# Moving the sample's early gate products in a two-layer diffusion backbone on one NeuronCore

## What is computed

```
proj = h @ w_in
attn = attention(...)                        # 8 heads
z    = short_conv(hy_in, width 3)            # 1536 channels: v, x1, x2 (512 each)
y    = v
for o in (0, 1):
    y = z[o + 1] * long_conv(y, filter[o])   # bidirectional, by a Fourier transform
g_a, g_b = split(sigmoid(gates))             # gates: 2 x 1024 columns of proj
merged = g_a * (attn @ w_oa) + g_b * (y @ w_ob)
x = x + gate1 * (merged @ w_out)
x = x + gate2 * peer(norm(x))                # 128 experts per token, fetched by index
```

## Time and profile before

| | us |
|---|---|
| median of three runs | 4868.67 |
| span of the profiled execution, first to last instruction | 4858.6 |
| median less span, what lies around it | 10.1 |
| TensorE busy | 3814.1 |
| VectorE busy | 3260.8 |
| layer 0, short convolutions begin to last gate product | 728.9 to 1106.3 |
| layer 1, the same | 2997.8 to 3360.0 |

### The profile page before, as it was taken

How to read it: one execution, slowest core, us unless ns; L and a number is a source line. 1 busy time by engine, 2 the same in 40 slices (tenths; PEclk the granted TensorE clock), 3 DMA queues, 4 the chain that set the end, 5 groups by cost and what they waited for, 6 DMA issues and landing times.

```text
span 4858.6 us, 42229 instructions
## 1 busy us (share of the span) xinstructions
PE 3814.1 (79%) x12642; PEld 2042.6 (42%) x12642; DVE 3260.8 (67%) x7651; ACT 1557.8 (32%) x4562; POOL 1793.3 (37%) x1515
## 2 busy tenths in 40 slices
PE   7987788797798766767877679799699777777776
PEld 4546464445454223323543346445555332322222
DVE  2323788858867986666567778876877876755555
ACT  2321241101234344434333323110233444444444
POOL 2330132333234434455344323224233444444443
PEclk8889889898899889898989889899799999999999
DMA  7565376766799989999999767766689999999998
GB/s 269 203 225 202 136 272 256 272 242 260 314 372 384 391 332 422 398 411 385 395 416 421 295 231 267 289 230 272 248 352 359 412 405 415 418 414 421 421 421 347
DMA packets 231264, 1602.62 MB, mean 330 GB/s; under 512 B 27558, under 2 KB 29906, under 8 KB 42876
## 3 DMA queue, kind: packets, MB, share of 16 engines
q0 software_dynamic: 198016, 1395.87, 72.4%
q1 hardware_dynamic: 33020, 204.06, 10.8%
HBM read 1588.52 MB, written 11.30 MB: 329 GB/s over the span
## 4 chain that ended last, share of the span: by engine, by line
PE 38%; DMA 28%; DVE 21%; issue 5%; ACT 5%; POOL 2%; SPq 0%; ACTq 0%; DVEq 0%; POOLq 0%
DMA sb_arena<-in_peer_uv,sb_idx 15%; PE ps L1133 14%; DMA sb_gbufs<-in_peer_uv,sb_idx 10%; PE ps L1029 7%; DVE sb_gbufs L1929 4%; PE ps L1070 4%; DVE sb_arena L1929 3%; DVE sb_eacc L1952 2%; PE ps L717 2%; PE ps L744 2%; PE ps L887 1%; DMA sb_ring<-in_w_oab 1%; DVE sb_arena L1915 1%; ACT sb_small L1393 1%; POOL sb_gbufs L2172 1%
## 5 line engine op out<-in xcount | busy, mean ns | idle before, releaser
L2172 POOL DMA_INDIRECT sb_gbufs<-in_peer_uv,sb_idx x768 | 981.9, 1279 | 1783.7 <-PE ps L1133 758.4
L1133 PE MATMUL ps<-sb_gbufs,sb_dge 128*128 128x512 f32 x1856 | 912.3, 641 | 281.5 <-ACT sb_dge L1413 274.0
L1133 PE MATMUL ps<-sb_arena,sb_dge 128*128 128x512 f32 x1856 | 902.4, 636 | 267.2 <-ACT sb_dge L1413 267.0
L2172 POOL DMA_INDIRECT sb_arena<-in_peer_uv,sb_idx x512 | 610.3, 1192 | 789.4 <-PE ps L1133 691.7
L1929 DVE CUSTOM_DVE_ANT_0 sb_gbufs<-sb_gbufs,sb_keep 128x1024 f32<-128x1024 f32 x512 | 625.6, 1235 | 355.7 <-DMA sb_gbufs<-in_peer_uv,sb_idx 352.5
L1929 DVE CUSTOM_DVE_ANT_0 sb_arena<-sb_arena,sb_keep 128x1024 f32<-128x1024 f32 x512 | 622.1, 1229 | 327.0 <-DMA sb_arena<-in_peer_uv,sb_idx 325.0
L1133 PEld LDWEIGHTS ps<-sb_gbufs,sb_dge 128*128 128x128 f32 x1856 | 363.1, 204 | 793.0 <-issue 392.3
L1133 PEld LDWEIGHTS ps<-sb_arena,sb_dge 128*128 128x128 f32 x1856 | 360.8, 202 | 777.2 <-issue 390.5
L1390 ACT ACTIVATE sb_small<-sb_small 128x2 f32<-128x2 f32 x512 | 104.1, 203 | 1516.3 <-DVE sb_small L1929 1491.1
L1952 DVE SCALAR_TENSOR_TENSOR sb_eacc<-sb_gbufs,sb_small,sb_eacc 128x1024 f32<-128x1024 f32 x299 | 387.3, 1295 | 7.8 <-DVE sb_small L1962 0.3
L1397 ACT ACTIVATE sb_small<-sb_small 128x1 f32<-128x1 f32 x1024 | 340.6, 379 | 49.6 <-ACT sb_small L1393 2.2
(11 more groups left out here) (272 smaller groups left out, 4276.7 us busy)
## 6 DMA issues: line engine op xcount, KB each, us to landing
sb_ring<-in_w_wq SPq DMA_DIRECT2D x48, 1024.0 KB
sb_keep<-in_w_ada POOLq DMA_DIRECT2D x52, 512.0 KB, 6.1
sb_ring<-in_w_hy SPq DMA_DIRECT2D x24, 1024.0 KB
sb_ring<-in_w_ga SPq DMA_DIRECT2D x16, 1024.0 KB
sb_ring<-in_w_gb SPq DMA_DIRECT2D x16, 1024.0 KB
sb_ring<-in_w_oab SPq DMA_DIRECT2D x16, 1024.0 KB
sb_ring<-in_w_out SPq DMA_DIRECT2D x14, 1024.0 KB
sb_gbufs<-in_peer_uv,sb_idx POOLq DMA_INDIRECT x768
```

Source lines behind the costliest of these rows:

```text
L1133: q = pe.matmul(ps[:, c, :], dge[:, b, :], gbuf[b][:, D + c * 512:D + c * 512 + 512], start=(h == 0 and i == 0), stop=(h == HALVES - 1 and ...
L2172: nc.gpsimd.indirect_dma_start(out=gbuf[b], out_offset=None, in_=I["peer_uv"], in_offset=bass.IndirectOffsetOnAxis(ap=idx[:, col:col + 1], ...
```

## The change

It changes the sample's dense steps alone.

- The first turning waits for four slices, not for eight, and comes after blocks 0 to 2 of the short convolution. Block 3 follows the first turning.
- The early gates (g_a and attn @ w_oa for c = 0, 1) come after the first inverse transform, before the second turning. Their tanh waits for the four results of the first order.
- Beside the second spectrum stand the products for g_b of c = 0 and 1 instead (new `early_second_gates`, banks 4 and 6), with their tanh.
- The gate step c = 0 then has the products of column 2 for g_a and g_b and (0, 3); step 1 has (1, 3) alone; step 2 has (2, 2) and (2, 3). The banks of the gate steps are shifted by four.
- Spectra 0 and 2 go to the arena too, and the load order is new. `w_oab` of columns 0 and 1 is loaded twice, the second time as `ob`: one more load of 1 MB for each layer.
- `pace` has new numbers; their sum falls from 933.8 to 899.8 us.

```diff
+def products_at(g, c):
+    if not g.latent or c > EARLY:
+        return [(c, q) for q in range(4)]
+    ahead = [(EARLY, 0), (EARLY, 1)]
+    return (ahead if c == 0 else []) + ([(c, 3)] if c < EARLY else [(c, 2), (c, 3)])
...
     def merge_bank(self, c, v):
-        return (4 * c + v) % 8 if self.latent else 2 + (4 * c + v) % 6
+        return (4 * c + 4 + v) % 8 if self.latent else 2 + (4 * c + v) % 6
...
-        at = [20 * k] + ... + [4.5] * (NH * nt) + [10] + [8 * k + 2] * (8 if self.latent else 12)
-        for o in (0, 1):
-            if self.latent:
-                at += [10] + [3.6] * 4 + ([10.5] * EARLY if o else [8] * 4) + [6] * 4
...
+        at = [20 * k] + ... + [4.5] * (NH * nt) + [10] + [8 * k + 2] * (6 if self.latent else 12)
+        if self.latent:
+            at += [4] + [8] * 2 + [3.6] * 4 + [8] * 4 + [3.5] * 4 + [10.5] * EARLY + [4] + [3.6] * 4 + [7.5] * EARLY + [3.5] * 4
...
-        return at + ([12] * EARLY + [21 * k + 2] * (8 - EARLY) if self.latent else ...
+        return at + ([20, 6, 8] + [21 * k + 2] * 5 if self.latent else ...
...
-            out += hy[0:4] + conv("MF", 0, "U_ps", 2) + conv("K", 0, "Ym", 1) + hy[4:5] + conv("K", 1, "Ym", 2, half) + hy[5:6]
-            out += conv("MI", 0, "y_ps", 4) + conv("MF", 1, "U_ps", 4) + conv("K", 2, "Ym", 3) + conv("K", 3, "Ym", 4, half)
-            out += [gates[0][0], gates[0][2]] + conv("MI", 1, "y_ps", 8) + [gates[0][1]]
+            out += hy[0:4] + conv("MF", 0, "U_ps", 2) + conv("K", 0, "Ym", 1, first) + conv("K", 1, "Ym", 2, half) + hy[4:6]
+            out += conv("MI", 0, "y_ps", 4) + [gates[0][0], gates[0][2]]
+            out += conv("MF", 1, "U_ps", 4) + conv("K", 2, "Ym", 3, first) + conv("K", 3, "Ym", 4, half)
+            out += [gates[0][1]] + conv("MI", 1, "y_ps", 8) + [((d, "ob", 0), 2048, None, free("mg_ps", gates_at(g, 1, 3)))]
...
-                yield from short_convolution(range(4 if g.latent else 6))
+                yield from short_convolution(range(3 if g.latent else 6))
...
-                    if g.latent:
-                        pe.wait_ge(*at("hyc", 12 if o else 8))
-                    else:
-                        pe.wait_ge(*at("hyc", 12))
+                    pe.wait_ge(*at("hyc", 4 if g.latent else 12))
...
+                def early_second_gates():
+                    pe.wait_ge(*loaded((d, "gb", 0)))
+                    w = weights((d, "gb", 0), 256)
+                    for c in range(EARLY):
+                        claim(4 + 2 * c, *at("eb_th", c + 1))
+                        for k in range(KD):
+                            m = pe.matmul(ps[:, 4 + 2 * c, :], w[:, k, c * 128:c * 128 + 128], v.hT[:, k, :], start=(k == 0), stop=(k == 7))
+                        m.then_inc(s["eb_ps"], 1)
+                        yield
...
                     turn_u(o)
                     yield
+                    if o == 0:
+                        yield from short_convolution((3,))
...
-                    if o:
-                        yield from early_gates()
-                    else:
-                        yield from short_convolution((4, 5))
+                    yield from early_second_gates() if o else short_convolution((4, 5))
...
+                    if o == 0:
+                        yield from early_gates()
...
+                    if g.latent and o == 0:
+                        act.wait_ge(*at("y", 4))
+                        for c in range(EARLY):
+                            act.wait_ge(*at("ea_ps", 2 * c + 1))
+                            act.activation(v.early[:, c, :], ps[:, 4 + 2 * c, :], ACT.Tanh, scale=0.5).then_inc(s["ea_th"], 1)
+                            yield
...
-                        if c >= 2:
-                            act.wait_ge(*at("mm", c - 1))
+                        if g.latent and cp < EARLY + 2:
+                            act.wait_ge(*at("y", 5 + 2 * (cp % 2) + q))
+                        elif cp >= 2:
+                            act.wait_ge(*at("mm", cp - 1))
```

More of the change, by code:

```diff
@@ L43 @@
 EARLY = 2
+def products_at(g, c):
[3 more added lines that the diff above has]
+    return (ahead if c == 0 else []) + ([(c, 3)] if c < EARLY else [(c, 2), (c, 3)])
 def gate_products(g):
-    return [(c, q) for c in range(KD) for q in range(4) if not (g.latent and c < EARLY and q % 2 == 0)]
+    return [p for c in range(KD) for p in products_at(g, c)]
 def gates_at(g, c, q):
@@ L169, in weight_loads @@
         hy = [((d, "hy", i), 2048, None, free("hyc_ps", 2 * i + 2)) for i in range(6)]
-        gates = [[((d, "ga", i), 2048, None, free("ea_ps", 3) if g.latent and 2 * i < EARLY else free("mg_ps", gates_at(g, 2 * i + 1, 0))),
-                  ((d, "gb", i), 2048, None, free("mg_ps", gates_at(g, 2 * i + 1, 1))),
-                  ((d, "oab", i), 2048, None, free("mg_ps", gates_at(g, 2 * i + 1, 3)))] for i in range(4)]
+        gates = [[((d, "ga", i), 2048, None, free("ea_ps", 3) if g.latent and i == 0 else free("mg_ps", gates_at(g, 2 * i + 1, 0))),
+                  ((d, "gb", i), 2048, None, free("eb_ps", 2) if g.latent and i == 0 else free("mg_ps", gates_at(g, 2 * i + 1, 1))),
+                  ((d, "oab", i), 2048, None, free("ea_ps", 4) if g.latent and i == 0 else free("mg_ps", gates_at(g, 2 * i + 1, 3)))] for i in range(4)]
         if g.latent:
@@ L1270, in short_convolution @@
                         yield
-                yield from short_convolution(range(8 if g.latent else 12))
+                yield from short_convolution(range(6 if g.latent else 12))
                 for o in (0, 1):
@@ L1715, in spectrum_s, with early_gates @@
                         yield from short_convolution(range(8, 12))
+                def early_gates():
+                    for c in range(EARLY):
+                        dve.wait_ge(*at("ea_th", c + 1))
+                        dve.wait_ge(*at("ea_ps", 2 * c + 2))
+                        dve.scalar_tensor_tensor(out=v.early[:, c, :], in0=v.early[:, c, :], scalar=1.0, in1=ps[:, 5 + 2 * c, :],
+                                                 op0=ALU.add, op1=ALU.mult).then_inc(s["ea"], 1)
+                        yield
                 for o in (0, 1):
@@ L1751, in dense @@
                 for c in range(KD):
-                    for q in (0, 1):
-                        if (c, q) not in gate_products(g):
-                            continue
-                        dve.wait_ge(*at("th", tanhs_at(g, c, q)))
+                    early = g.latent and c < EARLY
+                    for q in ((1,) if early else (0, 1)):
+                        dve.wait_ge(*(at("eb_th", c + 1) if early else at("th", tanhs_at(g, c, q))))
                         dve.wait_ge(*at("mg_ps", gates_at(g, c, 2 + q)))
@@ L2083, in dense @@
                     if g.latent:
-                        for _ in range(5 + (EARLY if o else 4)):
+                        for _ in range(5 + EARLY if o else 1 + 2 + 4 + 4):
                             yield
@@ L2094, in dense @@
                         yield
-                    for _ in range(4):
+                    for _ in range(4 + (EARLY if g.latent and o == 0 else 0)):
                         yield
```

62 lines of the change are left out of this document (31 added, 31 removed).

## The result

The changed kernel takes 4844.35 us (median of four runs, 4840.91 to 4856.21) and the kernel before 4869.34 beside it: the ratio is 0.995, with a 95% interval of 0.9932 to 0.9967. So it is faster, by 25.0 us. Run once more later it had 4850.21 against 4871.03, ratio 0.9954 (0.994 to 0.9967), which is 20.8 us. Both intervals stay clear of 1; between them they allow a gain of 16 to 33 us. The prediction was 4839.0 with a range of 4814 to 4861.

The account below looks back on a forecast made before the run. The stage was taken as a relay between PE and an almost full DVE. Gains of 28.1 (layer 0) and 15.6 us (layer 1), less 14 outside, gave 29.7 off: 4839.0 us, range 4814 to 4861.

Parts of the forecast that it names:

- The mechanism: Sample stage: filled PE holes bring the gates' end 28.1 us (layer 0) and 15.6 us (layer 1) earlier.
- ACT's copies: Behind the second turning: copies stand behind a unit's tanh in ACT's stream, a new PE wait of 10 to 15 us.
- First turning: Before the first inverse: holes of 4.95 and 8.45 us go; inverse at 829.6, was 845.35 (layer 1: 3098.1, was 3103.72).
- Gates: Second inverse's start to gates' end: inverse, products, rows and load waits sum to 158.1 us, was 181.9 and 177.2.
- The clock: Transform behind the second turning: half of the slow-clock loss, 1.5 us more in each layer, 3 in the sum.
- Outside: Attention and behind the gates: units moved there by the pace cost 4 and 3 us, 7 off for each layer.
- The full relay: Rival, second turning: unit burst hides beside the early gates, second spectrum starts right behind the turning; 4812.5 us, chance 0.12.
- The bound by the gathers: Rival, whole stage: DVE and gathers bind, filled holes open elsewhere; gain only 8 to 12 us, 4858, chance 0.19.
- That sign: Sample stage: DVE waiting on gathers for over 15 us would show the gather-bound or the slower rival.
- The sign of the span behind the gates: Behind the gates: that span growing by more than 6 us would show the prediction wrong.
- The slower case: Rival, burst behind the fourth result: gathers' cycle costs 3.0 us a unit, not 1.85, and the gain is gone; chance 0.08.
- The last rival: First turning: block 3 or early gates wait for reordered weight loads, turning no earlier; 4866 us, chance 0.05.

Follow-up runs that it names:

- the kernel with the moved burst: Changed kernel with the expert units behind the first order's fourth result moved later by the pace alone, same sum; 4837.31 us, ratio 0.9936.
- three relay kernels: Changed kernel with units moved by pace and ACT's copies ahead of early-gate units: 4827.54 us; plus new load order: 4824.19; plus 24 us more pace: 4816.66.
- the relay: Changed kernel with units behind the fourth result moved by pace and ACT's second-turning copies put ahead of the early gates' units; 4827.54 us, ratio 0.9913.

## Why the prediction was right, and where it was not

**The mechanism held.** The first turning is 19 us earlier relative to the convolution (60.1 to 41.2). The second stands with no hole ahead of it, at 864.2 and 3119.6. That 864.2 lies so near the forecast of 865.0 is luck: this execution was 4.9 us ahead when the convolution began (724.0, not 728.9), where 4 us of delay had been reckoned. Relative, the second turning came at 140.2 and 138.3, forecast 136.1 and 134.9. So it is 13.3 and 3.4 us earlier than before, and not 17.4 and 6.8. ACT's copies were forecast as a wait of 10 to 15 and took 14.05 and 12.30. From the second turning to the second inverse the sum said 55.1 and 53.6 us, and it was 54.2 and 53.5. The first products began at 72.6 relative, forecast 69.7.

**First turning: the spectrum's own wait was missed.** The sum let PE run from block 3 to 802 and on without a gap, and the text gave 3 us as the bound of any wait. The term that it put at nothing is the wait of the spectrum's second quarter for DVE's taps of block 3, which read the bank that PE writes next. It took 5.17 and 2.97 us. The first inverse came at 105.1 and 102.9 relative, where the sum has 100.7 and 100.3: 4.4 and 2.6 late. The move done alone shows the same wait at 11.48. This step failed, and the stage kept most of that lateness: 4.1 and 3.4 at the second turning, 3.2 and 3.3 at the second inverse.

**Gates: the sum of 158.1 was 2.3 and 1.7 short.** The second inverse ran in 16.20 and 16.93 (granted clock 0.87 and 0.83), not in 14.0, behind 7.87 and 9.39 us of wait. The product (2,2) ran in 8.80 in layer 0, not in 6.9. Against that the two waits on loads had been put at 0.8 and 5.9, and were 0.43 and 3.23 (0.46 and 3.26): the load of `oab` took 4.9 us from SP's issue to the product that waited for it, in both layers, not 7.64. In the kernel with the moved burst it took 7.9 and the wait was 6.20, near the forecast. So the clock was left out of this sum and the loads were put too dear, and the two errors partly cancel.

**The clock.** I took half of the loss for the transform behind the copies, 1.5 us. It ran in 16.35 and 15.94 at a granted clock of 0.85 and 0.87, so it lost 2.35 and 1.94. Behind 0.71 to 0.88 us of wait it ran in 14.00, at 1.00, in both layers of all three relay kernels. The Trainium skill, TensorE: Matmul & The Clock Gate, "What's actually happening", gives the slow start after idle; here these runs agree with it. The 14.00 behind the 23.07 us hole is no exception to that, if one looks one row further ahead. The rows of TensorE's windows for that turning and that transform (kernel before, layer 0):

```profile
882.00:886.00 4.00, 3.49 (x16) 3.28 (x16) 3.93 (x5) 1.87 (x4) 1.87 (x1) 0.55 0.94 346
886.00:900.50 14.50, 13.93 (x33) 6.28 (x34) 11.24 (x22) 1.81 (x4) 3.76 (x3) 1.00 0.80 293
```

The turning behind the hole was the slow one: 3.49 us at a granted clock of 0.55, where the changed kernel's took 2.15 at 1.00. (The rows know two levels, 0.50 and 1.00; what lies between is a stretch with both.) Then the clock was full. In layer 1 the turning ran at 0.50 and the transform behind it still at 0.85 (16.35 us). Both outcomes come up again: with the first turning moved alone, layer 1's turning took 3.66 and its transform 14.00; with the pace alone, layer 0's took 3.66 and 15.87. Which of the two an execution gets, no run here shows.

**Outside: the size was off by where it falls.** I put 4 us on each attention. Layer 0 paid nothing. Layer 1 paid 7.8: it took 222.1 and 222.3 us in the two kernels with the old sum of the pace, 224.1 with a sum of 923.8, and 225.1 to 232.9 in the nine profiles with 899.8. Behind the gates 3 and 3 became 3.5 and 5.5. That the sum of the pace sets this fits these twelve profiles, with one execution each; the nine alone differ by 7.8 us, so how much of it is the pace is less sure. Why layer 0's attention takes more units without cost was not settled.

**What made the total fit.** The span fell by 19.5 and not by 29.7. The two stages are 5.5 and 5.0 short, and that is all of the difference. Outside them the sum of 14 came out at 13.8 by luck: layer 1 took 3.8 more in the attention and 2.5 more behind the gates than forecast, layer 0's attention took 5.4 less, and 3.5 fell by chance ahead of all changed code. The median of four fell by 25.0, and the later one by 20.8, so the forecast of 29.7 was 5 to 9 too large. The mechanism was right in both stages, and the total lies near because its misses there were small; the outside terms fit only in their sum.

**Slips in the working.** The full relay's 877.3 and 3145.0 are when the second products would start, not the spectrum. For 3.0 us a unit the flights would have to be 17.3 us (24 less 6.7), not 19. By `pace` and `spread` layer 1's stage has 137 and 132 units, not 141 and 136; the difference of five, which the sum uses, is the same.

**The rivals.** The bound by the gathers (4858) is out: one edit of ACT's order and one of the pace gave 17 to 23 us more with the same gathers. DVE did wait on gathers for 22.9 and 23.0 us in the stage (17.7 and 15.8 before), more than the 15 that I had named as a sign of it. That sign was badly chosen, since the kernel before already exceeded it. The sign of the span behind the gates was left unclear: the stretch up to the experts grew by 5.5 us at most, under the bound of 6, but in layer 1 up to the kernel's end it is 7.6. The slower case did not come: from the fourth result to the last addition ahead of the second products DVE did 13 units and two dense multiplications of 0.68 in 21.5 us, which is 1.55 for a unit and not 3.0. Whether the loads slow the gathers was not tried. The last rival, reordered loads that come late for the turning, did not come either: the first turning stands at 41.2 in both layers, and no wait on a load stands ahead of either turning.

## What to carry to other kernels

In a relay between in-order engines, count for every hand-over what stands ahead of it in the receiver's stream, and what that in turn waits for. Here 2 us of copies stood 12 us behind two operations of 0.2 us, and reordering the receiver, with the background work moved out of the way, was worth nearly as much as the whole change. When a dense step gets shorter, the background work that was spread over it goes elsewhere; look for the stretch that pays for it. And when a wait is named in a trace, look for the next one hidden under it before its price is written down: of 5.73 us on a load, 2.80 were somebody else's too.

## What the runs showed that was not expected

- Executions of one kernel differ by 12 to 31 us between the quickest and the slowest (the relay: 4817.78 and 4848.81). The two profiles of the change are 19.7 us apart in the span, 8.8 of it in the long expert stretch (1516.0 and 1524.8 us). Over all twelve profiles that stretch lies between these two, whatever the edit.
- An execution takes only 1.8 us more than its span (4840.91 and 4839.1; 4860.62 and 4858.8).
- TensorE's transform costs 14.00 us behind 0.9 us of wait (granted clock 1.00) and 15.9 to 16.4 behind 12 to 14 (0.85 to 0.87); eight matmuls behind 6 us of wait on a load took 9.75 where 7.03 is usual.
